# Queries made transposed with stationary weights, and VectorE's low parts moved ahead of the score reductions

## The reference

```python
q = (c_q @ w_uq).reshape(B, S, MLA_HEADS, QK_NOPE + QK_ROPE)      # 256 -> 16 x (64 + 32)
q_nope = q[..., :QK_NOPE]
q_rope = apply_rope(q[..., QK_NOPE:], cos[:, :, None, :], sin[:, :, None, :])
k_rope = apply_rope(c_kv_full[..., KV_LORA:], cos, sin)           # one for all heads
kv = (c_kv @ w_ukv).reshape(B, S, MLA_HEADS, QK_NOPE + V_DIM)     # 128 -> 16 x (64 + 64)
s = (einsum("bqhd,bkhd->bhqk", qn, k_nope) + einsum("bqhr,bkr->bhqk", qr, k_rope)) * scale
p = softmax(where(mask, s, -inf))                                  # blocks of 128 queries
o = einsum("bhqk,bkhd->bqhd", p, v)
```

## Time and profile before

| | |
|---|---|
| median of three runs | 1139.03 us |
| the profiled execution | 1138.38 us, of it 1136.7 us span |
| TensorE, matmuls | 1109.6 us busy (98%), 5470 of them |
| TensorE, weight loads | 929.4 us (82%), beside the matmuls |
| VectorE | 867.9 us (76%) |
| ScalarE | 755.5 us (66%) |
| GpSimd | 35.1 us (3%) |
| chain that ended last | TensorE 77%, VectorE 18%, ScalarE 2% |

### The profile page before, as it was taken

How to read it: one execution, slowest core, us unless ns; L and a number is a source line. 1 busy time by engine, 2 the same in 40 slices (tenths; PEclk the granted TensorE clock), 3 DMA queues, 4 the chain that set the end, 5 groups by cost and what they waited for, 6 DMA issues and landing times.

```text
span 1136.7 us, 15525 instructions
## 1 busy us (share of the span) xinstructions
PE 1109.6 (98%) x5470; PEld 929.4 (82%) x5470; DVE 867.9 (76%) x1031; ACT 755.5 (66%) x941; POOL 35.1 (3%) x64
## 2 busy tenths in 40 slices
PE   9999999999999999999999999999999999999997
PEld 8888777888888888888777888887778887888885
DVE  6568666765554456468666779999999899999997
ACT  6555767455344345556667456799987898988785
POOL 3001000000000001001001000000000000000000
PEclk9999999999999999999999999999999999999999
DMA  8745523668555354646534648999999999999993
GB/s 321 280 147 185 174 92 109 218 216 304 184 185 185 111 184 139 218 132 189 171 103 138 199 169 282 390 401 412 415 418 366 382 404 408 406 415 400 417 371 143
DMA packets 120553, 294.94 MB, mean 259 GB/s; under 512 B 9007, under 2 KB 33677, under 8 KB 119965
## 3 DMA queue, kind: packets, MB, share of 16 engines
q1 hardware_dynamic: 119072, 288.23, 69.9%
q0 software_dynamic: 960, 5.28, 1.2%
q10 hardware_dynamic: 444, 0.47, 0.1%
HBM read 292.90 MB, written 1.05 MB: 259 GB/s over the span
## 4 chain that ended last, share of the span: by engine, by line
PE 77%; DVE 18%; ACT 2%; issue 2%; DMA 1%; ACTq 0%; DVEq 0%
PE bank L1739 22%; PE bank L1741 21%; PE bank L1740 21%; DVE w_lo L1514 10%; DVE w_lo_more L1514 3%; PE bank L2152 2%; PE bank L2153 2%; PE bank L1783 1%; PE bank L1955 1%; PE bank L1971 1%; PE bank L1963 1%; ACT w_hi L961 1%; DVE w_lo L1182 1%; PE bank L2135 1%; DVE hid_buf L1653 1%
## 5 line engine op out<-in xcount | busy, mean ns | idle before, releaser
L1182 DVE TENSOR_TENSOR w_lo<-raw,w_hi 128x1024 fp32r<-128x1024 f32 (+4 forms) x141 | 240.5, 1710 | 139.1 <-ACT w_hi L736 138.7
L736 ACT ACTIVATE w_hi<-raw 128x1024 fp32r<-128x1024 f32 (+5 forms) x141 | 201.4, 1432 | 151.8 <-PE bank L1741 151.8
L1514 DVE TENSOR_TENSOR w_lo<-raw,w_hi 128x1792 fp32r<-128x1792 f32 (+3 forms) x148 | 286.5, 1965 | 10.1 <-ACT w_hi L961 9.4
L961 ACT ACTIVATE w_hi<-raw 128x1792 fp32r<-128x1792 f32 (+3 forms) x148 | 244.0, 1668 | 43.0 <-PE bank L1741 31.1
L1739 PE MATMUL bank<-w_hi,aT_hi 128*128 128x512 f32 (+1 forms) x592 | 235.5, 398 | 0.6 <-DVE w_lo L1310 0.5
L1741 PE MATMUL bank<-w_hi,aT_lo 128*128 128x512 f32 (+1 forms) x592 | 229.6, 388 | 0.0
L1740 PE MATMUL bank<-w_lo,aT_hi 128*128 128x512 f32 (+1 forms) x592 | 229.6, 388 | 0.0
L1739 PEld LDWEIGHTS bank<-w_hi,aT_hi 128*128 128x128 f32 x592 | 111.2, 188 | 24.2 <-issue 3.2
L1741 PEld LDWEIGHTS bank<-w_hi,aT_lo 128*128 128x128 f32 x592 | 111.2, 188 | 22.8
L1740 PEld LDWEIGHTS bank<-w_lo,aT_hi 128*128 128x128 f32 x592 | 111.3, 188 | 20.2
L1514 DVE TENSOR_TENSOR w_lo_more<-raw,w_hi_more 128x1792 fp32r<-128x1792 f32 (+3 forms) x50 | 96.7, 1941 | 4.6 <-ACT w_hi_more L961 4.6
(11 more groups left out here) (328 smaller groups left out, 1787.9 us busy)
## 6 DMA issues: line engine op xcount, KB each, us to landing
raw<-in_moe_w_gate SPq DMA_DIRECT2D x128, 448.0 KB, 6.5
raw<-in_moe_w_up SPq DMA_DIRECT2D x128, 448.0 KB, 6.4
raw<-in_moe_w_down SPq DMA_DIRECT2D x112, 512.0 KB, 6.5
raw<-in_w_in SPq DMA_DIRECT2D x40, 768.0 KB, 4.4
raw<-in_dense_w_gate SPq DMA_DIRECT2D x22, 512.0 KB, 3.8
raw<-in_dense_w_up SPq DMA_DIRECT2D x22, 512.0 KB, 4.6
raw<-in_dense_w_down SPq DMA_DIRECT2D x11, 1024.0 KB, 4.9
raw<-in_w_in SPq DMA_DIRECT2D x20, 512.0 KB, 4.8
```

Source lines behind the costliest of these rows:

```text
L736: act.activation(dst, src, ACT.Copy).then_inc(hi_made[j], 1)
L961: act.activation(split_of(hi_slot, m), raw_of(i, n), ACT.Copy).then_inc(e_hi_made, 1)
L1182: dve.tensor_tensor(dst, src, high, ALU.subtract).then_inc(lo_made[j], 1)
L1514: dve.tensor_tensor(split_of(lo_slot, m), raw_of(i, n), split_of(hi_slot, m).bitcast(F32), ALU.subtract).then_inc(e_lo_made, 1)
```

## The change

The queries' columns are loaded in another order: slab 0 now holds the 32 rotary columns of all 16 heads, slabs 1 and 2 the 64 other columns of eight heads each, each load in two DMAs with runs of 128 or 256 bytes where the rows before were 2048 bytes. TensorE makes slab 0 token-major (12 matmuls of 512 columns) and slabs 1 and 2 transposed with stationary weights like the keys (48 matmuls of 256 columns). The result is copied to `qT`, which now holds all heads on 128 partitions, by ScalarE (even heads) and VectorE (odd heads, no longer moved across partitions). An even head has its 64 plain rows above and its rotary rows below, an odd head the other way; the remaining 32 rows of the keys are zero. The rotary columns go to `q_rope`, with two heads swapped in place, are rotated by VectorE, and are transposed four heads at a time (eight transposes in all, after the convolution's block); four copies by ScalarE and four by VectorE bring them in. The transposes and the copy of one head per step leave the loop. The scores alternate between banks 4 and 5 and contract over 128 rows. On VectorE the low parts and the biases take new places in the loop, ahead of the step's masked maximum. GpSimd zeroes four stretches and spreads the rotary key in eight copies instead of two, and VectorE makes four copies of the rotary key from PSUM instead of one.

```diff
+LOW_PART_AT = {6 * g + s: (BLK_GATE + g + 1, j) for g in range(2) for s, j in ((3, 0), (6, 1), (7, 2))}
+LOW_PART_AT.update({HEADS + 1: (BLK_CONV1, 0), HEADS + 2: (BLK_CONV1, 1)})
+BIAS_AT = {8: 1, 14: 2}
...
-                    load(b, j, B, [(slot(b, j, 2, NB), chunks(w_uq[L])[:, :, j * NB:(j + 1) * NB])])
+                    heads_uq = chunks(w_uq[L]).rearrange("p c (h d) -> p c h d", d=QK)
+                    part = heads_uq[:, :, :, NOPE:QK] if j == 0 else heads_uq[:, :, (j - 1) * HEADS // 2:j * HEADS // 2, 0:NOPE]
+                    dst = slot(b, j, 2, NB).rearrange("p c (h d) -> p c h d", d=part.shape[3])
+                    load(b, j, B, [(dst[:, c], part[:, c]) for c in range(2)])
...
+                for n in range(4):
+                    last = pool.memset(rope_k2[n * ROPE:(n + 1) * ROPE, 1 - n % 2, :], 0.0)
+                link(last)
                 for dst in (kT, kT_last):
-                    pool.tensor_copy(dst[NOPE:QK, :, :], k_ropeT[NOPE:QK, :].unsqueeze(1).to_broadcast(
-                        [ROPE, dst.shape[1], S])).then_inc(k_rope_spread, 1)
+                    groups = dst[:, :, :].rearrange("p (b y x) s -> p x b y s", y=2, x=2)
+                    for x, rows in ((0, slice(NOPE, P)), (1, slice(0, NOPE))):
+                        for b in range(dst.shape[1] // 4):
+                            last = pool.tensor_copy(groups[rows, x, b], rope_k2[rows, :, :])
...
-                act.wait_ge(heads_ready, 4 * (L + 1))
+                for n in range(4):
+                    act.wait_ge(q_tr, 2 * L + n // 2 + 1)
+                    act.activation(queries_of(n)[0:NOPE, 1:4:2, :],
+                                   bank[B_QR[n // 2]][0:NOPE, n % 2 * S:(n % 2 + 1) * S].unsqueeze(1).to_broadcast([NOPE, 2, S]),
+                                   ACT.Copy).then_inc(qk_act, 1)
...
                 for n in range(HEADS + 3):
-                    if n < HEADS:
-                        act.wait_ge(q_tr, HEADS * L + n + 1)
-                        if n:
-                            act.wait_ge(s_made, HEADS * L + n)
-                        act.activation(qT[0:QK, :], bank[B_QK][0:QK, 0:S], ACT.Copy).then_inc(q_in, 1)
...
+                lo(B + BLK_UKV, 0, UKV_SIZES[0], True)
+                odd_queries_in(L, 0)
+                odd_queries_in(L, 1)
+                lo(B + BLK_UKV, 1, UKV_SIZES[1], True)
+                odd_queries_in(L, 2)
+                odd_queries_in(L, 3)
+                lo(B + BLK_UKV, 2, UKV_SIZES[2], True)
...
                 los(L, BLK_GATE)
+                for n in range(4):
+                    dve.wait_ge(q_tr, 2 * L + n // 2 + 1)
+                    dve.tensor_copy(queries_of(n)[NOPE:2 * NOPE, 0:4:2, :],
...
                         dve.tensor_scalar(p_buf[:, P:3 * P], p_buf[:, P:3 * P], row_inv[:, 1:2], None, ALU.mult).then_inc(p_scaled, 1)
+                    if n in LOW_PART_AT and n <= HEADS + 1:
+                        b, j = LOW_PART_AT[n]
+                        lo(B + b, j, SLAB_SIZES[j])
+                    if n in BIAS_AT:
+                        add_bias(BIAS_AT[n])
                     if 1 <= n <= HEADS:
...
-                        if n - 1 in GRANULE_AHEAD:
-                            b, j = GRANULE_AHEAD[n - 1]
-                            lo(B + b, j, SLAB_SIZES[j])
...
-                    if n in (GATE_SLOTS, 2 * GATE_SLOTS):
-                        add_bias(n // GATE_SLOTS)
...
+            def queries(L, n, j):
+                for x in range(2):
+                    for c in range(2):
+                        at_col = c * NB + (n % 2 * 2 + x) * P
+                        pair, s = slice(at_col, at_col + P), weight_slot(MIX[L], j)
+                        last = product(keys_bank(n)[:, x * S:(x + 1) * S], w_hi[:, s, pair], w_lo[:, s, pair],
+                                       lT_hi[:, c, :], lT_lo[:, c, :], c == 0, c == 1)
+                return last
+
+            def transpose_rotary(L):
+                pe.wait_ge(heads_ready, 4 * (L + 1))
+                pe.wait_ge(qk_act, keys_in(L, 3))
+                pe.wait_ge(qk_dve, keys_in(L, 3))
+                for n in range(4):
+                    for t in range(NT):
+                        last = pe.transpose(bank[B_QR[n // 2]][:, n % 2 * S + t * P:n % 2 * S + (t + 1) * P],
+                                            q_rope[:, t, 4 * n:4 * n + 4, :].rearrange("p h d -> p (h d)"), ident[:, :])
...
                 slab(L, BLK_CONV, PAIR_CONV, bT_hi, bT_lo, first_chunk=L + 2)
+                transpose_rotary(L)
...
-                        for t in range(NT):
-                            last = pe.transpose(bank[B_QK][0:QK, t * P:(t + 1) * P], q[:, t, n * QK:(n + 1) * QK], ident[:, :])
-                        last.then_inc(q_tr, 1)
...
-                        if n >= 2:
-                            pe.wait_ge(max_made, 2 * (HEADS * L + n - 1))
+                        if n >= 3:
+                            pe.wait_ge(max_made, 2 * (HEADS * L + n - 2))
```

More of the change, by code:

```diff
@@ L1356, in mixer @@
                         dve.wait_ge(k_rope_tr, L + 1)
-                        dve.tensor_copy(k_ropeT[NOPE:QK, :], bank[B_LT + 1][0:ROPE, S:2 * S]).then_inc(k_rope_in, 1)
+                        for n in range(4):
+                            last = dve.tensor_copy(rope_k2[n * ROPE:(n + 1) * ROPE, n % 2, :], bank[B_LT + 1][0:ROPE, S:2 * S])
+                        last.then_inc(k_rope_in, 1)
                     if p == 3:
@@ L1386, in mixer @@
                 lo(B + BLK_UQ, 2, UQ_SIZES[2])
-                for j in range(3):
-                    lo(B + BLK_UKV, j, UKV_SIZES[j], True)
+                lo(B + BLK_UKV, 0, UKV_SIZES[0], True)
[5 more added lines that the diff above has]
+                lo(B + BLK_UKV, 2, UKV_SIZES[2], True)
                 move_keys(L, 0)
@@ L1823, in keys @@
                 return last
+            def queries(L, n, j):
+                for x in range(2):
+                    for c in range(2):
[8 more added lines that the diff above has]
+                pe.wait_ge(qk_dve, keys_in(L, 3))
+                for n in range(4):
+                    for t in range(NT):
+                        last = pe.transpose(bank[B_QR[n // 2]][:, n % 2 * S + t * P:n % 2 * S + (t + 1) * P],
+                                            q_rope[:, t, 4 * n:4 * n + 4, :].rearrange("p h d -> p (h d)"), ident[:, :])
+                    if n % 2:
+                        last.then_inc(q_tr, 1)
             def mixer(L):
@@ L1890, in mixer @@
                 slab(L, BLK_GATE0, PAIR_GATE0, aT_hi, aT_lo, after_granule_0=transpose_b)
-                for j in range(3):
-                    pe.wait_ge(lo_made[j], MIX[L] + BLK_UQ + 1)
-                    for t in range(NT):
-                        wait_pair_free(pe, L, PAIR_UQ + j, t)
-                        for c in range(2):
-                            last = product(bank[2 * ((PAIR_UQ + j) % 2) + t][:, :], tile(lT_hi, c, t), tile(lT_lo, c, t),
-                                           w(L, j, c, NB, NB, w_hi), w(L, j, c, NB, NB, w_lo), c == 0, c == 1)
-                        if t == 0:
-                            last.then_inc(out_made, 1)
-                    last.then_inc(used[j], 1)
+                pe.wait_ge(lo_made[0], MIX[L] + BLK_UQ + 1)
+                for t in range(NT):
+                    wait_pair_free(pe, L, PAIR_UQ, t)
+                    for c in range(2):
+                        last = product(bank[2 * (PAIR_UQ % 2) + t][:, :], tile(lT_hi, c, t), tile(lT_lo, c, t),
+                                       w(L, 0, c, NB, NB, w_hi), w(L, 0, c, NB, NB, w_lo), c == 0, c == 1)
+                    if t == 0:
+                        last.then_inc(out_made, 1)
+                last.then_inc(used[0], 1)
+                pe.wait_ge(prod_made, 4 * (L + 1))
+                for j in (1, 2):
+                    pe.wait_ge(lo_made[j], MIX[L] + BLK_UQ + 1)
+                    queries(L, 2 * j - 2, j).then_inc(qk_made, 1)
+                    queries(L, 2 * j - 1, j).then_inc(used[j], 1)
                 pe.wait_ge(lo_made[0], MIX[L] + BLK_UKV + 1)
-                pe.wait_ge(prod_made, 4 * (L + 1))
                 for n in range(2):
-                    keys(L, n, 0, 2 * n).then_inc(keys_made, 1)
+                    keys(L, n, 0, 2 * n).then_inc(qk_made, 1)
                 for t in range(NT):
```

116 lines of the change are left out of this document (76 added, 40 removed).

## The result

The changed kernel takes 1143.59 us (median of five runs, 1142.92 to 1144.37) against 1139.03 before, a ratio of 1.0039 with a 95% interval of 1.0029 to 1.0050. It is slower by 4.6 us. The forecast was 1142.7. The profiled execution took 1143.57 us, of it 1141.8 us span.

What follows compares the result with a forecast made beforehand. TensorE's own list was taken as the bound. Per layer, +0.78 ahead of the loop and +1.03 in it made 1.8 us, 3.6 for two layers: 1142.0 profiled, 1142.7 us median; range 1135.5 to 1146.0.

Steps and rivals of the forecast that it cites:

- Queries: Ahead of the head loop: TensorE's query matmuls take 8.44 us per layer instead of 8.16, +0.28.
- First scores: Ahead of the loop: VectorE's rotary copies and TensorE are ready almost together, 129.35 against 129.32; up to +0.5 as bound.
- Chain of head 1: Start of the loop: head 1's scores through maximum and exponential to its transposes take 3.36 us.
- Loop: From head 1's transposes (T1) to head 15's (T15): new waits outweigh the transposes removed, +1.03 us per layer.
- T13 to T15: Loop, start of head 13's transposes to start of head 15's: 6.42 us where it was 6.82, -0.40.
- Waits: In the loop, TensorE's waits for divided numerators grow from 1.9 to about 6 us per layer, longest 1.4 to 1.7.
- Low parts hidden: Rival: in the loop VectorE finishes the low parts before scores come; -3.1 us per layer, 1132.8 us; chance 0.13.
- Halfway: Rival: the loop's waits grow by about half of the forecast, as ScalarE may run ahead; 1137.8 us; chance 0.19.
- Short runs late: Rival: query slab loads in 128 or 256 byte runs land 10.6 us late per layer; 1160 us; chance 0.06.
- GpSimd's copies: Ahead of the loop: spreading the rotary key in eight copies costs nothing, any hold-up being inside VectorE's slack.
- T1 to T3: Loop, start of head 1's transposes to start of head 3's: 7.58 us where it was 7.27, +0.31.
- T5 to T7: Loop, start of head 5's transposes to start of head 7's: 7.14 us where it was 6.45, +0.69.

Runs made afterwards that it cites:

- rotary_first: Changed kernel with VectorE's four copies of the transposed rotary columns ahead of the first gate block's last low part: 1142.34 us.
- low_tiny: Changed kernel with the loop's low parts ahead of the maximum cut to 8 columns each, the other columns not computed: 1134.38 us.
- before_low_ahead: Kernel before the change, with only VectorE's order changed: low parts and biases ahead of the masked maximum: 1142.05 us.
- low_late: Changed kernel with VectorE's old order in the head loop put back, low parts behind the masked maximum, queries staying changed: 1138.35 us.
- one_bank: Changed kernel with one scores bank in place of two, each head's scores waiting for the maximum of the head before: 1143.02 us.

## Why the prediction was right

**Step by step.** The layer was to be 1.8 us longer and is 2.0.

- *Queries*, +0.28: from the first query matmul (99.17) to the convolution block's end (124.25) it is 25.08 us against 24.76, +0.32.
- *Eight rotary transposes*, 0.93 with the change back to split products: 124.25 to 125.04, 0.79 in all. A little too dear.
- *First scores at 5.04 us after the block's end, a draw*: they came at 5.27. Here the sum was short. The copies start 2.61 us after the block's end (126.86), where 1.35 + 1.23 had 2.58, and take 2.52 until 129.38, just as 2.44 + 0.08 had it. But these terms add up to 129.41 and not to the 129.35 that the sum gave, and the scores start 0.14 after the last copy's end, for which it had nothing: 0.03 + 0.06 + 0.14. So it was no draw: VectorE was last by 0.3 us, as rotary_first shows, within the bound of 0.5.
- *Chain of head 1*, 3.36 from the earlier trace rows: it took 3.44. Queries +0.04, first scores +0.23 (the cheaper transposes do not help, as VectorE was last) and this chain +0.08 make the front 0.35 us per layer longer than forecast; this is the term that was mis-sized, +1.13 where I had +0.78.
- *Loop*, +1.03: measured +0.86. The first four gaps, three of them chains put together from single rows and T3 to T5 TensorE's own work, held to 0.01 us, and T9 to T13 to 0.03. T13 to T15 was 0.12 too long in my sum.
- *After T15*: unchanged, 6.02 against 6.01.
- *Waits*: 5.7 us per layer where I had about 6, the marks 1.22 to 1.47 where I had 1.4 to 1.7. The low parts of steps 3, 7, 9 and 13 wait 1.00, 0.57, 1.00 and 0.57 us for ScalarE's `w_hi`, those of steps 6 and 12 not at all, as forecast.

Front and loop together miss by 2 x (0.35 - 0.17) = 0.4 us. The rest of the 0.9 us between 1142.7 and 1143.59 is not in the attention: from the second layer's second convolution block to the end the profiled executions of all ten kernels take between 523.66 and 525.95 us, before 523.87, after 525.03, with no order by kernel. Held against the profiled executions alone, the forecast was further off: 1142.0 against 1143.57 us, 0.4 of it in the attention and 1.2 in that last stretch. The prediction had put nothing there, so the 0.9 us by which the medians missed is in part luck.

**The rivals.** *Low parts hidden*: excluded, and its price roughly confirmed by low_tiny, which comes near that case. It gave 1134.38 us where the rival had 1132.8, and its gaps 6.51, 7.16, 6.07 and 7.50 stand against 6.53, 7.20, 6.07 and 7.43 in the prediction; the 1.6 us too many lie mostly in the front (+0.35 per layer) and in T13 to T15 (6.30 against 6.07). *Halfway*: the worst links do chain; ScalarE without its 15 copies does not run ahead. Its exponential ahead of the high part (133.61) follows 0.65 after the transposes of head 1 (132.96), and 1.26 later comes the high part, as in the earlier trace rows. *Short runs late*: excluded by the DMA rows, first after, then before (the loads of `w_ukv` are of the same 256 KB, but in runs of 2048 bytes):

```profile
DMA packets 135497, 294.95 MB, mean 258 GB/s; under 512 B 25486, under 2 KB 50156, under 8 KB 134908
...
raw<-in_w_uq SPq DMA_DIRECT2D x12, 256.0 KB, 3.6
...
raw<-in_w_ukv SPq DMA_DIRECT2D x4, 256.0 KB, 2.9
```

```profile
DMA packets 120553, 294.94 MB, mean 259 GB/s; under 512 B 9007, under 2 KB 33677, under 8 KB 119965
...
raw<-in_w_uq SPq DMA_DIRECT2D x6, 512.0 KB, 3.5
```

There are 16,479 more packets under 512 bytes. A load in short runs lands 0.7 us later than one of the same size in long runs, and about as late as one of twice its size did before. The Trainium skill, page "DMA: Bandwidth & Descriptors", section "Specifications", asks for 512 bytes a transfer for the full rate. These rows agree in so far as the short runs are slower; whether anything is read and written twice no row shows. But the first slab has 20.2 us until it is read, before and after (issued at 70.64, read from 90.86), its reader again waits for TensorE and not for the load, and so the rule costs nothing here. I had priced the three slabs of a layer at up to 42.4 us; their six loads take 6 x 3.6 = 21.6 us even if none overlapped, under the 32 from which it would have decided.

**GpSimd's copies**, priced at nothing. GpSimd and VectorE while the rotary key is spread:

```profile
99.44 4.55 POOL L739 COPY kT<-rope_k 64x512 f32<-64x512 f32 x6
...
104.03 2.17 POOL L739 COPY raw<-rope_k 64x512 f32<-64x512 f32 x2
...
100.52 1.23 DVE L1239 TENSOR_TENSOR w_lo<-raw,w_hi 128x1024 fp32r<-128x1024 f32 x1
...
103.72 1.34 DVE L1239 TENSOR_TENSOR w_lo<-raw,w_hi 128x1024 fp32r<-128x1024 f32 x1 [1.98 <-ACT w_hi L772]
```

The same subtraction that took 2.29 us beside one long copy takes 1.23 and 1.34 beside short ones. The waiting has moved to GpSimd: six of its eight copies take 0.61 us, but the one that begins at 100.56, 0.04 behind the first subtraction, takes 1.67, and the one that begins at 104.03, 0.31 behind the second, takes 1.52. The Trainium skill, page "SBUF — State Buffer", section "SBUF: two separate sides", has GpSimd and a VectorE instruction with two SBUF inputs exclude each other for a whole instruction. The rows agree: both slow copies end 0.5 us after the subtraction that they met. The subtractions are held up for 0.11 us at most, where beside the one long copy it was over 1 us. The price of nothing was right.

**Where I was wrong in the experiments.** For before_low_ahead I let TensorE's extra 0.43 us per two heads hide the lateness, and came to 0.7 us where the loop grew by 1.55. In T1 to T3 and T7 to T9 it hides nothing: these gaps are as long as in the changed kernel (+0.31 and +0.59 over before), and only the wait within them is shorter. In T5 to T7, and again in T11 to T13, it hides a part: 6.89 us against 7.13 and 7.12 in the changed kernel, still 0.44 and 0.45 over before.

## What to carry to other kernels

When work is moved in front of a step on an in-order engine, look first at when its own input is made: here the move cost 5.2 us (low_late against the changed kernel), and with the input made one step earlier the same place was 2.1 us faster than low_late. Work that is taken from the busiest engine is worth nothing in a gap that a chain sets: T1 to T3 took 7.58 us with two pairs of transposes more and 7.59 without them. So go gap by gap, take for each the later of the engine's own work and the chain, and sum the differences; and look for an order in which the chain starts earlier (the scores ahead of the chunks gave 5.7 us), before cutting more work.

## What the runs showed that I had not expected

- Chain gaps repeat between kernels: T7 to T9 takes 8.79, 8.79, 8.79 and 8.80 us in after, before_low_ahead, one_bank and rotary_first. The least steady gap of the three with the changed queries, T5 to T7, is 7.13, 7.18 and 7.11. So a difference of 0.1 us in a stretch can be told from a single trace, where the whole times of one kernel spread by 0.6 to 2.5 us.
- The part of the program that no kernel changed took 523.66 to 525.95 us in the ten profiled executions. A forecast of a single execution carries that spread, however good its sum is; for the medians, twice the difference in "whole" missed the time by up to 0.7 us.
